# A fourteen-block fp32 network on one core: transposing x before its norm is known, with filler matmuls between the groups of transposes

## The reference

```
x = x + hybrid(rmsnorm(x))          # attention and Mamba-2 side by side; twice, each followed by
x = x + swiglu(rmsnorm(x))          #   down(silu(h @ gate) * (h @ up)), hidden width 2816
x = rmsnorm(x, final_norm)
for i in range(4):                  # mixers A, B, C, A
    x = x + rms_norm(0.5 * swiglu_2(rms_norm(x)))      # the 0.5 sits in the scale of the sum of squares
    x = x + rms_norm(mixer_i(rms_norm(x)))
    x = x + rms_norm(0.5 * swiglu_2(rms_norm(x)))
```

## Time and profile before

| | us |
|---|---|
| median of three runs | 3002.1 (3000.1 to 3004.4) |
| span of the profiled execution | 3003.8 |
| TensorE busy | 2797.4 (93%) |
| TensorE weight loads | 2578.4 (86%) |
| VectorE busy | 1567.4 (52%) |
| ScalarE busy | 1316.3 (44%) |
| GpSimd busy | 162.7 (5%) |
| DMA | 457 MB, mean 152 GB/s |

### The profile page before, as it was taken

How to read it: one execution, slowest core, us unless ns; L and a number is a source line. 1 busy time by engine, 2 the same in 40 slices (tenths; PEclk the granted TensorE clock), 3 DMA queues, 4 the chain that set the end, 5 groups by cost and what they waited for, 6 DMA issues and landing times.

```text
span 3003.8 us, 50257 instructions
## 1 busy us (share of the span) xinstructions
PE 2797.4 (93%) x19530; PEld 2578.4 (86%) x19530; DVE 1567.4 (52%) x1868; ACT 1316.3 (44%) x1929; POOL 162.7 (5%) x229
## 2 busy tenths in 40 slices
PE   6889999799999979999998899999998999997998
PEld 6778999689889968999998589999987999996898
DVE  4655446654554555455454645454555545455544
ACT  4534445344444444444444544444454444444443
POOL 0000000100000010000000300000011000001000
PEclk9989999899999999999998999999999999999999
DMA  5325644066746425656645046656444665652564
GB/s 161 114 83 164 184 144 144 16 187 184 208 145 182 141 80 174 183 168 189 183 151 177 1 145 185 196 160 183 139 162 121 188 196 156 182 152 80 168 183 131
DMA packets 575818, 457.00 MB, mean 152 GB/s; under 512 B 19276, under 2 KB 537956, under 8 KB 575716
## 3 DMA queue, kind: packets, MB, share of 16 engines
q1 hardware_dynamic: 573124, 453.47, 50.5%
q10 hardware_dynamic: 2560, 2.10, 0.3%
q0 software_dynamic: 32, 0.02, 0.0%
HBM read 452.37 MB, written 1.07 MB: 151 GB/s over the span
## 4 chain that ended last, share of the span: by engine, by line
issue 67%; PE 20%; DVE 4%; POOL 3%; ACT 2%; DVEq 1%; POOLq 1%; DMA 1%; ACTq 0%; SPq 0%
PE gu L782 2%; PE gu L784 2%; PE gu L783 2%; PE acc L627 2%; PE gu L596 1%; POOL arena L1005 1%; PE gu L619 1%; PE gu L615 1%; PE gu L614 1%; POOL small L455 1%; DVE lo_a L422 1%; POOLq L454 1%; PE gu L790 1%; PE gu L789 1%; PE gu L788 1%
## 5 line engine op out<-in xcount | busy, mean ns | idle before, releaser
L422 DVE TENSOR_TENSOR lo_a<-raw_a,hi_a 128x2048 fp32r<-128x2048 f32 x313 | 711.7, 2274 | 550.3 <-ACT hi_a L410 550.3
L615 PE MATMUL gu<-xT_lo,hi_a 128*128 128x256 f32 x3360 | 824.3, 283 | 0.0
L614 PE MATMUL gu<-xT_hi,hi_a 128*128 128x256 f32 x3360 | 822.9, 283 | 0.0
L615 PEld LDWEIGHTS gu<-xT_lo,hi_a 128*128 128x128 f32 x3360 | 644.3, 192 | 7.8
L614 PEld LDWEIGHTS gu<-xT_hi,hi_a 128*128 128x128 f32 x3360 | 643.4, 191 | 7.8
L410 ACT ACTIVATE hi_a<-raw_a 128x2048 fp32r<-128x2048 f32 x313 | 592.8, 1894 | 76.6 <-PE acc L627 58.6
L654 ACT ACTIVATE arena<-gu 128x256 f32<-128x256 f32 x220 | 84.7, 385 | 986.5 <-PE gu L619 957.3
L619 PE MATMUL gu<-xT_hi,lo_a 128*128 128x256 f32 x3360 | 471.7, 283 | 0.0
L619 PEld LDWEIGHTS gu<-xT_hi,lo_a 128*128 128x128 f32 x3360 | 433.4, 192 | 0.0
L671 DVE TENSOR_TENSOR arena<-arena,gu 128x256 f32<-128x256 f32 x220 | 92.8, 422 | 641.1 <-ACT arena L654 641.1
L627 PE MATMUL acc<-hi_b,h_hi 128*128 128x512 f32 x880 | 274.2, 393 | 1.0 <-DVE h_lo L675 1.0
(11 more groups left out here) (256 smaller groups left out, 3374.4 us busy)
## 6 DMA issues: line engine op xcount, KB each, us to landing
raw_a<-in_ffn_w_in SPq DMA_DIRECT2D x352, 512.0 KB, 5.6
raw_b<-in_ffn_w_out SPq DMA_DIRECT2D x176, 512.0 KB, 3.6
raw_a<-in_w_in SPq DMA_DIRECT2D x52, 512.0 KB, 4.8
raw_a<-in_w_gate SPq DMA_DIRECT2D x44, 512.0 KB, 4.8
raw_a<-in_w_up SPq DMA_DIRECT2D x44, 512.0 KB, 6.1
raw_b<-in_w_down SPq DMA_DIRECT2D x44, 512.0 KB, 3.6
raw_a<-in_w_out SPq DMA_DIRECT2D x24, 512.0 KB, 4.3
raw_a<-in_c_w_in SPq DMA_DIRECT2D x24, 512.0 KB, 4.6
```

The source lines that it names most:

```text
L422: nc.vector.tensor_tensor(a_view(lo_a, par)[:, :, 0:width], a_view(raw_a, par)[:, :, 0:width], a_view(hi_a, par)[:, :, 0:width].bitcast(F3 ...
L614: nc.tensor.matmul(o, w, xT_hi[:, kt, :], start=(kt == 0), stop=False)
L615: nc.tensor.matmul(o, w, xT_lo[:, kt, :], start=False, stop=False)
```

## The change

It takes rstd out of the path to the transposes, in every stage but the final norm.

- **Raw x is transposed.** x is added in four quarters (token half, column half) with a semaphore for each; TensorE transposes each quarter as it comes. The sum of squares of x and rstd are made after ScalarE's copies. rstd then goes into a diagonal matrix (VectorE), TensorE multiplies it by ones so that every partition holds the row of all rstd (`rows_pe`, behind the first products), and ScalarE copies that to `rb`.
- **rstd is put in later.** In an FFN, VectorE multiplies the gate half by `rb` before silu, one more operation per tile; the up half stays unscaled, which the norm behind it absorbs through its eps (second part) or the addition to x undoes (first part). In the mixers VectorE copies the projections with hidden units on partitions out of PSUM, times `rb`; ScalarE keeps those with tokens on partitions.
- **Fillers.** 16 matmuls before the transposes (20 before) and 6 after each of the first three groups of four, at the seams where x comes from a stage before; after the final norm only the latter.
- **The stage's end** goes by quarters: the four banks of `acc` are finished one after another, also in the last output slot of a mixer, and the squares, gains and additions are done on 512 columns each.
- **The low part of slot 1** of the next stage moves from before the stage's end to behind `xT_lo`, and the hybrids' fourth conv tap is taken from the copy in SBUF by ScalarE, after the slot's split.

```diff
+WARM_PRE = 16
+WARM_TURN = 6
         def pre_pe(pe, s):
-            if s.k:
-                if stages[s.k - 1].kind != "final":
-                    keep_warm(20)
-                pe.wait_ge(x_ready, 2 * s.k)
-            turn_pe(pe, s.turn0, xn)
+            if s.k and stages[s.k - 1].kind != "final":
+                keep_warm(WARM_PRE)
+            for t in range(NT):
+                for h in range(2):
+                    wait_x(pe, s, t, h)
+                    if s.k == 0 and t == 0 and h == 0:
+                        pe.wait_ge(bias_row_ready, 1)
+                    for kt in range(4 * h, 4 * h + 4):
+                        mm = nc.tensor.transpose(turn_bank[:, t, h, kt % 4, :], x[:, t, kt * P:(kt + 1) * P], ident)
+                    mm.then_inc(turned, 1)
+                    if s.k and 2 * t + h < 3:
+                        keep_warm(WARM_TURN)
+        def pre_act(act, s):
...
+                    for kt in range(4 * h, 4 * h + 4):
+                        ins = nc.scalar.activation(xT_hi[:, kt, t * P:(t + 1) * P], turn_bank[:, t, h, kt % 4, :],
+                                                   ACT.Copy, scale=col(kt))
+                    ins.then_inc(turn_hi, 1)
+            for t in range(NT):
+                wait_x(act, s, t, 1)
+                act.drain()
+                nc.scalar.activation(junk, x[:, t, :], ACT.Square, scale=D ** -0.5, accum_out=ssx[:, t:t + 1]).then_inc(sq_act, 1)
+        def rows_act(act, s):
+            act.wait_ge(rb_ps, s.pre + 1)
+            nc.scalar.activation(rb, tp[:, 1, 0:256], ACT.Copy).then_inc(rb_ready, 1)
+        def pre_dve(dve, s):
...
+                for kt in range(4 * h, 4 * h + 4):
+                    ins = nc.vector.scalar_tensor_tensor(by_t(xT_lo[:, kt, :]), turn_bank[:, :, h, kt % 4, :],
+                                                         col(kt), by_t(xT_hi[:, kt, :].bitcast(F32)), ALU.mult, ALU.subtract)
+                ins.then_inc(turn_lo, 1)
+            ahead_a(lo_slot_a, dve, s.a0 + 1)
+            dve.wait_ge(rstdx_ready, s.pre + 1)
+            if s.kind == "ffn" and added_norm(s):
+                nc.vector.tensor_scalar(eps_y, ssx, EPS2, 4 * EPS2, ALU.add, ALU.mult)
...
+            for t in range(NT):
+                ins = nc.vector.tensor_scalar(diag[:, t, :], ident, rstdx[:, t:t + 1], None, ALU.mult)
+            ins.then_inc(diag_ready, 1)
+        def rows_pe(pe, s):
+            pe.wait_ge(diag_ready, s.pre + 1)
+            for t in range(NT):
+                mm = nc.tensor.matmul(tp[:, 1, t * P:(t + 1) * P], ones, diag[:, t, :], start=True, stop=True)
+            mm.then_inc(rb_ps, 1)
         def post_act(act, s):
...
+                for c in range(2):
+                    wait_out(act, s, t, c)
+                    nc.scalar.activation(junk[:, c * 512:(c + 1) * 512], acc[:, 2 * t + c, :], ACT.Square, scale=scale,
+                                         accum_out=ssy[:, 2 * t + c:2 * t + c + 1]).then_inc(post_sq, 1)
         def ffn_pe(pe, s):
             pre_pe(pe, s)
             ffn_in_pe(pe, s, s.a0, s.b0, s.a0 % 2, 0, first=True)
+            rows_pe(pe, s)
             ffn_in_pe(pe, s, s.a0 + 1, s.b0 + 1, (s.a0 + 1) % 2, 1)
         def ffn_tile_act(act, n, m, pa, pm, more_a, more_b):
-            act.wait_ge(a_used, n + 1)
+            act.wait_ge(hid_scaled, m + 1)
...
-            nc.scalar.activation(sg[:, pm, :], gu[:, pm, 0:256], ACT.Silu).then_inc(hid_gate, 1)
+            nc.scalar.activation(sg[:, pm, :], gs[:, pm, :], ACT.Silu).then_inc(hid_gate, 1)
         def ffn_tile_dve(dve, n, m, pa, pm, more_a, more_b):
+            dve.wait_ge(a_used, n + 1)
+            nc.vector.tensor_tensor(gs[:, pm, :], gu[:, pm, 0:256], rb, ALU.mult).then_inc(hid_scaled, 1)
             dve.wait_ge(hid_gate, m + 1)
...
             if more_b:
                 lo_slot_b(dve, m + 1, 1 - pm)
-            elif more_a:
-                lo_slot_a(dve, n + 2, par=pa)
         def ffn_act(act, s):
             pre_act(act, s)
+            rows_act(act, s)
             ffn_tiles(act, s, hi_slot_b, ffn_tile_act)
         def ffn_dve(dve, s):
             pre_dve(dve, s)
+            dve.wait_ge(rb_ready, s.pre + 1)
             ffn_tiles(dve, s, lo_slot_b, ffn_tile_dve)
         def out_split(split, eng, s, slots=None):
...
+                if split is lo_slot_a and r == n_out - 1:
+                    continue
```

More of the change, by code:

```diff
@@ L63 @@
 SLOT = 2048
-SMALL = 1152
+SMALL = 804
 SLOT_B = 1024
@@ L153 @@
 KINDS = {
[L155 to L158, removed]
+    "hybrid": (14, 20, 4, 4),
+    "A": (5, 9, 8, 8),
+    "B": (11, 19, 16, 8),
+    "C": (12, 16, 8, 8),
 }
@@ L574, in post_dve @@
                 dve.drain()
-                dve.wait_ge(rstd_ready, 2 * e + 1 + t)
-                nc.vector.scalar_tensor_tensor(x[:, t, :], xn[:, t, :], rstd[:, o:o + 1], x[:, t, :],
-                                               ALU.mult, ALU.add).then_inc(x_ready, 1)
+                for c in range(2):
+                    nc.vector.scalar_tensor_tensor(half(x, t, c), half(xn, t, c), rstdy[:, t:t + 1], half(x, t, c),
+                                                   ALU.mult, ALU.add).then_inc(x_ready[t], 1)
@@ L733, in load_gain @@
         def load_gain(sp, s, row):
-            sp.wait_ge(x_ready, 2 * (s.k - (s.kind == "final")))
+            for t in range(NT):
+                sp.wait_ge(x_ready[t], 2 * (s.k - 1 if s.kind == "final" else s.k))
             sp.dma_start(gain_b, row.partition_broadcast(P)).then_inc(gain_full, 16)
@@ L791, in proj_pe, with proj_done, evacuate, scaled @@
             mm.then_inc(a_used, 1)
-        def proj_act(act, s, i, evacuate):
+        def proj_done(eng, p):
+            eng.wait_ge(proj_out[p % 2], p // 2 + 1)
+        def evacuate(eng, s, i, copy):
             n, p = s.a0 + i, s.proj0 + i
-            act.wait_ge(a_used, n + 1)
-            evacuate(gu[:, p % 2, :]).then_inc(proj_out, 1)
-            ahead_a(hi_slot_a, act, n + 2)
+            eng.wait_ge(a_used, n + 1)
+            copy(gu[:, p % 2, :]).then_inc(proj_out[p % 2], 1)
+        def scaled(out, bank, rows=slice(0, P)):
+            n = out.shape[1]
+            return nc.vector.tensor_tensor(out, bank.rearrange("p (u t) -> p u t", u=n),
+                                           rb[rows, :].unsqueeze(1).broadcast_to([out.shape[0], n, SEQ]), ALU.mult)
+        def by_token(out, bank, func=ACT.Copy, factor=None):
+            for t in range(NT):
+                ins = nc.scalar.activation(out[:, t, :], bank[:, t, :], func, scale=(rstdx if factor is None else factor)[:, t:t + 1])
+            return ins
         def out_pe(pe, s, slots):
@@ L1631, in final_pe @@
         def final_pe(pe, s):
-            pe.wait_ge(x_ready, 2 * s.k)
+            for t in range(NT):
+                pe.wait_ge(x_ready[t], 2 * s.k)
             pe.wait_ge(scratch_in, 16)
@@ L1765, in _ @@
                         nc.gpsimd.tensor_tensor(rstd[:, o], ms[:, o], mhalf[:, 0:2], ALU.pow).then_inc(rstd_ready, 1)
-                elif s.kind != "final" and added_norm(s):
-                    rms_pow_pool(pool, s.rms0 + 1, (4 if s.kind == "ffn" else 1) * EPS2)
+                if added_norm(s):
+                    for t in range(NT):
+                        pool.wait_ge(sumy_ready, 2 * s.post + t + 1)
+                        nc.gpsimd.tensor_tensor(rstdy[:, t:t + 1], sumy[:, t:t + 1], mhalf[:, 0:1], ALU.pow).then_inc(rstdy_ready, 1)
         @block.scalar
```

402 lines of the change are left out of this document (235 added, 167 removed).

## The result

The changed kernel took **3028.8 us** (median of four runs, 3025.3 to 3033.0), the kernel before, on the same chip, 3002.1 (3000.1 to 3004.4): a ratio of **1.0079, interval 1.0062 to 1.0096**. It is slower, as forecast, but by 26.7 us where 10.6 had been summed, and it lies above the range. The profiled execution (3025.3, span 3023.5) is the fastest of the four; before, the span was 3003.8. All medians here are over fast runs; one run of the kernel before (4030.9 us) and one of the seventh experiment (11271.9 us) were slow and are not counted.

The account below looks back on a forecast made before the run. TensorE was taken as busy nearly all the time, so the change could win only at seams. Seam, launch and attention terms, including new FFN waits, summed to +10.6 us on 3002.1, thus 3012.7 us; range 2989 to 3023.

Parts of the forecast that it names:

- The wait at out 0: Before each FFN's first output product, TensorE waits 2.4 us for `h_lo`, in ten FFNs; 24 us in all.
- The seams: Between stages: slot 1 at 16.8 us after the fillers start, for 16.54 before, FFN to FFN; fillers set the pace.
- the wait for the diagonal: Before slot 1, TensorE waits 0.7 us for rstd's diagonal, as GpSimd is blocked by VectorE's split.
- the launch: At the kernel's start, slot 1 comes at 33.9 us for 37.39: -3.5 us.
- the price of the clock: Behind the new wait in ten FFNs: clock loss priced at 0, with an upper end of 0.64 us each.
- Rival C: The clock falls in the new waits or fillers don't hold it: +0.64 x 10, 3019.1 us; chance 0.12.
- A's attention: In mixer A, the last projection's copy stands behind a score on VectorE: 0.5 us each, +1.0 in all.
- The fillers hold the clock through a seam: At the seams, fillers between groups of transposes keep TensorE at 2.4 GHz; this is in the sums.
- The next tile catches up: In each FFN, the tile after the first gets a whole further slot, so the lateness of 2.4 us ends there.
- Rival A: The wait before the first output product does not arise, the chain from rstd matmuls to `h_lo` under 5.8: 2988.7 us; chance 0.16.

Follow-up runs that it names:

- the seventh experiment: Both reorderings of the first tile on the changed kernel: slot b 0 split ahead of `rb`, hidden tile split ahead of slot a 2; 2990.4 us, 0.9950.
- one reordering alone: Changed kernel with slot b 0 split ahead of `rb` on ScalarE and VectorE; 3005.1 us, ratio 1.0008 against the kernel before.
- h first: Changed kernel with `h_hi` and `h_lo` ahead of the split of slot a 2 in each FFN's first tile; 3006.7 us, ratio 1.0007.
- five fillers with the order in A: Changed kernel with five fillers ahead of each FFN's first output product and A's last projection copied out before its second score; 3019.0 us, 1.0046.

## Why the prediction was wrong in size

- **The wait at out 0: right.** Forecast 2.4 in ten FFNs and 20 to 25 us at that releaser; 2.24 and 24.1.
- **The seams: right within 2 us for each kind.** Slot 1 at 16.57 for 16.8; the wait for the diagonal 0.32 for 0.7; x ready at 4.8 for 5.8 behind an FFN; behind a mixer out 0 at 26.45 to 26.6 in three and 28.75 in the fourth, for 26.6. Two sums of the prediction are off by a tenth: the last copy ends at 10.7, not 10.8, and three operations of 0.2 behind 15.6 end at 16.2, not 16.35; measured were 16.1. GpSimd did meet VectorE's split (1356.70 to 1358.98), and rstd was there 0.9 behind its end, 0.8 as assumed. Its row answers to the earlier trace rows:

```profile
1357.64 1.39 POOL L1747 TENSOR_SCALAR small<-small 128x2 f32<-128x2 f32 x1 [9.95 <-ACT arena L543]
1359.18 0.70 POOL L1749 TENSOR_TENSOR small<-small 128x2 f32<-128x2 f32 x1
```

  At the launch slot 1 came at 35.16 for 33.9; in the profiles of the experiments, whose launch is the same program, it lies between 33.9 and 35.5.
- **The failed step is the price of the clock.** I took "2.31 idle alone left the next operations at full pace" from the earlier trace rows and priced the wait at 0, at most 0.64. Those operations lasted only 1.06 and then paused. Three profiles have fifteen falls behind out 0. In four of them the first product is already slow, in eleven the first one wholly at half pace starts 0.4 to 1.6 us after the work resumes. In the earlier trace rows the second group of transposes, 1.5 us after the work resumes, is slow as well: those rows had the fall, just behind the stretch that I read. The 0.64 was what a fall had left to cost in slot 0; with dense products behind it a fall costs 1.6. Ten fillers in the wait gave back 10.8 of the 16.1 that were missing (9.6 by the ratios). Rival C had the mechanism and a price 2.5 times too small.
- **A's attention: too small.** 0.5 each was taken, as between nothing and one operation in a queue. The copy really stands behind a whole softmax step on VectorE, which itself waits for scores that TensorE makes behind the last projection: it starts 5.6 us after TensorE has left that slot (1081.40 against 1075.81), with the copy first 0.1 us after. A's stretch to the first output product grew by 1.8 and 2.3, and with the copy first the growth was gone. C grew by 1.1, which I had not priced.
- **"The fillers hold the clock through a seam": right behind FFNs, not always behind mixers.** Behind the last A the first transposes waited 2.08 and the fillers ran at half pace: first product at 13.2 for 10.9, 2.3 us in one seam.
- **The next tile catches up: right** for the change; when `h_lo` went first, the next tile had the wait.
- **Rival A** needed the chain under 5.8 against 8.0; with both reorderings it is, and the time, 2990.4, is close to its 2988.7.

With the 10.8 that ten fillers gave back and the two mixer terms as measured the sum is 10.6 + 10.8 + 1.7 (A) + 1.1 (C) = 24.2 of 26.7 us. The rest is smaller than what the hybrids and B differ by between kernels, and is not assigned; for the same reason the closeness is not a proof of each term.

## What to carry to other kernels

A wait of TensorE has two prices: its length, and the clock behind it; a wait of 2 us between dense products can cost 1.6 more, so price it both ways, taking the whole stretch that would run slow and not the part of it that happens to be left in a nearby row. When a deferred scale moves the chain behind the first tile, move the operand splits out of that chain on both engines, and look at the tile after as well: of 24.1 us of wait one reordering alone left 6.9, the other 9.5 at the tile after, both 1.8. Fillers pay as far as they lie in a wait that exists anyway; count them against the engine that sets the pace, here ScalarE's sixteen copies.

## What the runs showed of the hardware

- **A fall of the clock after the same idle is not certain.** In the three profiles with an idle of 2.24 to 2.26 ahead of out 0 in ten FFNs, it fell in 4, 5 and 6 of them (six, three and no fillers between groups), each time at a cost of about 1.6 us, the worth of eight products; in four of the fifteen the first product already lasted 0.68 to 0.80. In the profiles with 1.14 or less there it fell in none. The 1.79 shown above was followed by a fall, the 1.60 at out 1 with h first was not. Here are two FFNs of the changed kernel, the same idle and no fall, then a fall:

```profile
2838.68 0.50 PE L684 MATMUL acc<-hi_b,h_hi 128*128 128x512 f32 x1 [2.25 <-DVE h_lo L735]
2839.02 0.39 PE L684 MATMUL acc<-lo_b,h_hi 128*128 128x512 f32 x1
...
2840.18 0.39 PE L684 MATMUL acc<-hi_b,h_hi 128*128 128x512 f32 x1
```
```profile
1167.24 0.50 PE L684 MATMUL acc<-hi_b,h_hi 128*128 128x512 f32 x1 [2.25 <-DVE h_lo L735]
...
1168.56 0.63 PE L684 MATMUL acc<-hi_b,h_lo 128*128 128x512 f32 x1
```

  The Trainium skill, "TensorE: Matmul & The Clock Gate", section "A second HAM failure mode: psum-queue depth-cycling", says that short idles that recur between groups of matmuls can make the clock swing between its levels; the trace agrees that short idles can do it, and shows that one of 2.24 to 2.26 between dense stretches was enough in 15 of 30 cases.
- **A mean clock that is higher than before went with a longer time**: 0.975 against 0.966. The mean says how the clock stood over the whole span, not what the slow stretches held up: the old seams ran transposes at half speed, the new waits have dense products behind them. That reading is argued; no run separates it.
- **One kernel's runs differ with the clock**: five fillers with the order in A took 3008.5 at a mean of 0.979 and 3023.3 at 0.971.
- **The first product behind a wait for `h_lo` lasts 0.50 for 0.40**, and FFNs take 175.57 for 175.47 from there. It isn't the idle that costs this 0.1: with ten fillers in the wait and 0.02 of idle left the product lasts 0.50 and the FFNs take 175.57 to 175.62 as well. What does is not shown.
